# A decoder kernel's first output projection, from one f32 product to three f16 products, with its operands halved during the recurrence solve

## The reference, cut to what matters

```
xn   = rms_norm(x) ; proj = xn @ w_in                      # 1024 -> 3336 columns
y_ssd  = ssd_mixer(proj[:, :1544])                         # 512 columns, a chunked state space mixer
y_rwkv = rwkv7_mixer(proj[:, 1544:])                       # 512 columns, a delta-rule recurrence of 8 heads
mix  = concat(y_ssd, y_rwkv) @ w_out                       # (256 x 1024) @ (1024 x 1024)
h    = x + rms_norm(mix) * post_mix_norm
h    = h + rms_norm(ffn(rms_norm(h)))                      # width 2816, gated, with a short convolution
```

## Time and profile before

| | |
|---|---|
| median of 3 executions | 862.06 us (860.3 to 863.2) |
| the profiled execution | 863.93 us, its span 862.1 us |
| busy, PE / PEld / DVE / ACT / POOL | 815.8 / 688.3 / 565.1 / 391.2 / 71.5 us |
| SP's waits for the first projection's and the second's slots (L438 on L598) | 153.0 us in four waits |
| PE granted clock, stretches of the solve | 0.57 of full in 190 to 194, 1.00 in 174 to 178 |

### The profile page before, as it was taken

One profiled execution on the slowest core, in us unless ns is written; L12 is line 12 of the kernel. 1 busy time (PEld: TensorE's weight loads), 2 busy tenths in 40 slices (PEclk: granted clock), 3 DMA queues, 4 the chain that ended last, 5 costly groups with the idle time before them and its releaser, 6 DMA issues.

```text
span 862.1 us, 17113 instructions
## 1 busy us (share of the span) xinstructions
PE 815.8 (95%) x7466; PEld 688.3 (80%) x7466; DVE 565.1 (66%) x881; ACT 391.2 (45%) x613; POOL 71.5 (8%) x98
## 2 busy tenths in 40 slices
PE   4999978988999999999999999999998999999996
PEld 3798866777767788888886868597886888888885
DVE  2769975645166889999856777567457566674443
ACT  3546351120053376666754764116256356653333
POOL 1123011202000211111000100000200200000000
PEclk9999996998799999999999999979999999999999
DMA  9772230203004745555586256100482516555201
GB/s 329 290 294 98 98 110 2 101 2 102 1 1 156 272 158 196 195 196 197 195 299 240 98 210 227 52 2 0 177 313 99 194 67 227 196 196 209 86 2 49
DMA packets 66491, 127.93 MB, mean 148 GB/s; under 512 B 3696, under 2 KB 27504, under 8 KB 66288
## 3 DMA queue, kind: packets, MB, share of 16 engines
q1 hardware_dynamic: 65104, 122.92, 39.6%
q0 software_dynamic: 592, 2.69, 0.9%
q10 hardware_dynamic: 720, 1.23, 0.4%
HBM read 125.78 MB, written 1.05 MB: 147 GB/s over the span
## 4 chain that ended last, share of the span: by engine, by line
PE 74%; DVE 15%; ACT 6%; issue 2%; DMA 2%; POOL 0%; DVEq 0%; SPq 0%; ACTq 0%
PE bank L493 21%; PE bank L601 18%; DVE arena L481 7%; PE bank L598 6%; PE bank L699 6%; DVE arena L1865 3%; PE bank L1162 3%; PE bank L1953 3%; DMA ring<-in_w_in_dram 2%; ACT arena L472 2%; PE bank L1414 1%; PE bank L1181 1%; PE bank L2335 1%; PE bank L2077 1%; PE bank L2092 1%
## 5 line engine op out<-in xcount | busy, mean ns | idle before, releaser
L481 DVE SCALAR_TENSOR_TENSOR arena<-ring,arena 128x1024 f16<-128x1024 f32 x194 | 229.5, 1230 | 75.7 <-ACT arena L472 75.3
L493 PE MATMUL bank<-hg,arena 128*128 128x256 f16 x2496 | 275.1, 273 | 1.0 <-DVE arena L481 1.0
L493 PEld LDWEIGHTS bank<-hg,arena 128*128 128x128 f16 x2496 | 243.2, 98 | 32.4 <-issue 2.5
L472 ACT ACTIVATE arena<-ring 128x1024 f16<-128x1024 f32 x194 | 191.9, 1045 | 83.5 <-PE bank L601 51.8
L601 PE MATMUL bank<-arena 128*128 128x256 f16 x1296 | 142.2, 273 | 0.2 <-DVE arena L481 0.2
L601 PEld LDWEIGHTS bank<-arena 128*128 128x128 f16 x1296 | 126.6, 98 | 15.5 <-issue 0.9
L598 PE MATMUL bank<-mix,ring 128*128 128x256 f32 x256 | 55.7, 379 | 1.1 <-ACT arena L1797 1.1
L699 PE MATMUL bank<-hg,ring 128*128 128x256 f32 x224 | 51.5, 391 | 4.7 <-DMA ring<-in_w_in_dram 4.7
L598 PEld LDWEIGHTS bank<-mix,ring 128*128 128x128 f32 x256 | 48.5, 190 | 8.4 <-issue 1.9
L699 PEld LDWEIGHTS bank<-hg,ring 128*128 128x128 f32 x224 | 43.7, 197 | 11.4 <-DMA ring<-in_w_in_dram 5.1
L508 ACT ACTIVATE hg<-h,params 128x256 f16<-128x256 f32 (+1 forms) x48 | 23.9, 499 | 56.4 <-DVE h L2281 42.8
(11 more groups left out here) (365 smaller groups left out, 964.7 us busy)
## 6 DMA issues: line engine op xcount, KB each, us to landing
ring<-in_w_in_dram SPq DMA_DIRECT2D x13, 2048.0 KB, 8.7
ring<-in_ffn_w_up_dram SPq DMA_DIRECT2D x22, 1024.0 KB, 7.4
ring<-in_w_ff_dram SPq DMA_DIRECT2D x8, 2048.0 KB, 9.0
ring<-in_w_ff_dram SPq DMA_DIRECT2D x16, 1024.0 KB, 6.0
ring<-in_ffn_w_down_dram SPq DMA_DIRECT2D x11, 1024.0 KB, 6.3
ring<-in_w_out_dram SPq DMA_DIRECT2D x8, 1024.0 KB, 6.3
ring<-in_w_xk_dram SPq DMA_DIRECT2D x2, 2048.0 KB, 12.0
ring<-in_w_xv_dram SPq DMA_DIRECT2D x2, 2048.0 KB, 8.3
```

The costliest lines, as they stand in the source:

```text
L472: nc.scalar.activation(quarter(halves_of(chunk)[0], chunk, q), quarter(slot(*chunk), chunk, q), ACT.Copy, scale=W_SCALE).then_inc(*mark("w ...
L481: nc.vector.scalar_tensor_tensor(quarter(halves_of(chunk)[1], chunk, q), quarter(slot(*chunk), chunk, q), W_SCALE, quarter(halves_of(chunk ...
L493: mm = nc.tensor.matmul(out_, weight[a][:, k, cols], src[:, k, b, :], start=(first and i == 0), stop=(last and i == 2), skip_group_check=True)
```

## The change

The projection `w_out` is now three f16 products per tile, as elsewhere. Its weights are cut in eight row tiles q, each of 128x1024, by `out1_high` (ACT) and `out1_low` (DVE), which stand inside the two chunks of the solve: q = 4c, 4c+1, 4c+2, 4c+3 in chunk c. The halves of q = 0 and 4 go into `hg`, which is free there; those of the others take the place of the f32 words of the tile before, so `out1_high(q)` waits for `out1_low(q - 1)`. ACT's list alternates `mem_high` and `out1_high`. DVE's has `out1_low(4c)` after level 0, `out1_low(4c + 1)` after level 2, `out1_low(4c + 2)` after the 64-wide join, and `out1_low(4c + 3)` after the RK masks. In chunk 1 the mix tiles 0 to 3 are cut as well (`act_mix1_high`, `dve_mix1_low`), into the place of row tile 3. At the end of the recurrence, tiles 4 to 7 are cut from Y: DVE's gate product stays in f32, ACT makes the high half, DVE the low half, the first pair's low half standing inside DVE's work for the second pair. The post norm's root takes the constant that goes with a result 64 times as large.

```diff
--- before.py
+++ after.py
@@ -566,6 +566,45 @@
             mm.then_inc(*mark("column_rstd", n, "column"))
 
 
+        def out1_words(q):
+
+            return ring[:, CHUNK_NO[("w_out", "rows", q // 4)] % RING, 1024 * (q % 4):1024 * (q % 4) + 1024]
+
+        def out1_halves(q):
+
+            kept = hg[:, q:q + 4, :].rearrange("p k t -> p (k t)") if q in (0, 4) else out1_words(q - 1)
+            return kept.bitcast(F16).rearrange("p (w n) -> p w n", w=2)
+
+        def out1_high(act, q):
+            if q % 4 == 0:
+                act.wait_ge(*at("chunk", CHUNK_NO[("w_out", "rows", q // 4)]))
+                act.wait_ge(*at("proj1", PBANKS - 1))
+            else:
+                act.wait_ge(*at("out1 weights low", q - 1))
+            nc.scalar.activation(out1_halves(q)[:, 0, :], out1_words(q), ACT.Copy, scale=W_SCALE).then_inc(
+                *mark("out1_weights_high", "out1 weights high", q))
+
+        def out1_low(dve, q):
+            dve.wait_ge(*at("out1 weights high", q))
+            nc.vector.scalar_tensor_tensor(out1_halves(q)[:, 1, :], out1_words(q), W_SCALE, out1_halves(q)[:, 0, :],
+                                           ALU.mult, ALU.subtract).then_inc(
+                *mark("out1_weights_low", "out1 weights low", q))
+
+        ssd16 = out1_words(3).bitcast(F16).rearrange("p (k w t) -> p k w t", k=4, w=2)
+        mix1_16 = [ssd16[:, k] if k < 4 else mix16[:, k] for k in range(KT)]
+
+        def act_mix1_high(act):
+            act.wait_ge(*at("mix1", 3))
+            act.wait_ge(*at("out1 weights low", 3))
+            nc.scalar.activation(ssd16[:, :, 0, :], mix[:, 0:4, :], ACT.Copy).then_inc(*mark("mix1_high", "mix1 high", 3))
+
+        def dve_mix1_low(dve):
+            dve.wait_ge(*at("mix1 high", 3))
+            nc.vector.tensor_tensor(ssd16[:, :, 1, :], mix[:, 0:4, :], ssd16[:, :, 0, :], ALU.subtract).then_inc(
+                *mark("mix1_low", "mix1 low", 3))
+            for k in range(3):
+                same(("mix1 low", k), ("mix1 low", 3))
+
         def wide(pe, chunk, j, bank, half):
 
             if chunk in SPLIT_NO:
@@ -594,6 +633,11 @@
                 out_, cols = halves(4 + m // 2)[:, m % 2, :], slice(m * P, (m + 1) * P)
                 first = i == order[0] and kk == 0 and m % 2 == 0
                 last = i == order[-1] and kk == min(4, ktiles - 4 * i) - 1
+                if name == "w_out":
+                    for n, (a, b) in enumerate(((0, 0), (1, 0), (0, 1))):
+                        mm = nc.tensor.matmul(out_, out1_halves(k)[:, a, cols], mix1_16[k][:, b, :],
+                                              start=(first and n == 0), stop=(last and n == 2), skip_group_check=True)
+                    return mm
                 if not split:
                     return nc.tensor.matmul(out_, slot(name, "rows", i)[:, kk, cols], src[:, k, :], start=first,
                                             stop=last, skip_group_check=True)
@@ -610,6 +654,8 @@
                 by_rows = n - 2 if tail else n
                 for kk in range(n):
                     pe.wait_ge(*at(*src_ready(4 * i + kk)))
+                    if name == "w_out":
+                        pe.wait_ge(*at("out1 weights low", 4 * i + kk))
                     if split:
                         pe.wait_ge(*at("low", SPLIT_NO[(name, "rows", i)], kk))
                     if kk < by_rows:
@@ -1616,6 +1662,8 @@
                         *mark("solve_vector", "X", c, g, n + 1))
                 if n in (1, 3):
                     mem_low(dve, 4 * c + n // 2 + 2)
+                if n in (0, 2):
+                    out1_low(dve, 4 * c + n // 2)
                 if n == 3:
                     dve_mem_keys(dve, 2 * c)
             for g in range(2):
@@ -1640,6 +1688,7 @@
                                       banks[3 * g][64:128, 0:256].rearrange("p (j m) -> p j m", j=4)).then_inc(
                     *mark("solve_vector", "P64", c, g))
             mem_low(dve, 4 * c + 4)
+            out1_low(dve, 4 * c + 2)
 
             for g in range(2):
                 dve.wait_ge(*at("AK bank", c, g))
@@ -1654,6 +1703,9 @@
                 dve.wait_ge(*at("RK bank", c, g))
                 nc.vector.tensor_tensor(sets[g]["RK"], quarters(3 * g), over(const("incl"), 4), ALU.mult).then_inc(
                     *mark("solve_vector", "RK", c, g))
+            out1_low(dve, 4 * c + 3)
+            if c:
+                dve_mix1_low(dve)
             for g in range(2):
                 dve.wait_ge(*at("RB bank", c, g))
                 nc.vector.tensor_tensor(sets[g]["ARB"], quarters(3 * g + 2), over(const("neg_incl"), 4),
@@ -1670,8 +1722,12 @@
             mem_low(dve, 4 * c + 5)
 
         def act_rwkv_chunk(act, c):
-            for n in range(4 * c + 2, 4 * c + 5):
-                mem_high(act, n)
+            for i in range(3):
+                mem_high(act, 4 * c + 2 + i)
+                out1_high(act, 4 * c + i)
+            out1_high(act, 4 * c + 3)
+            if c:
+                act_mix1_high(act)
             for g in range(2):
                 st = sets[g]
                 act.wait_ge(*at("G bank", c, g))
@@ -1755,6 +1811,13 @@
                     *mark("bonus_vector", *(("bonus products",) if j == 3 else ())))
 
         def dve_rwkv_end(dve):
+            def mix1_low(i):
+                dve.wait_ge(*at("mix1 high", 4 + 2 * i))
+                nc.vector.tensor_tensor(mix16[:, 4 + 2 * i:6 + 2 * i, 1, :], Y[:, 2 * i:2 * i + 2, :],
+                                        mix16[:, 4 + 2 * i:6 + 2 * i, 0, :], ALU.subtract).then_inc(
+                    *mark("rwkv_end_vector", "mix1", 4 + 2 * i))
+                same(("mix1", 5 + 2 * i), ("mix1", 4 + 2 * i))
+
             for i in range(2):
                 dve.wait_ge(*at("mean bank", i))
                 nc.vector.scalar_tensor_tensor(flat(Y)[:, 512 * i:512 * i + 512], banks[4 + i][:, :], -1.0 / RW_HD,
@@ -1772,6 +1835,8 @@
                 dve.wait_ge(*so_far("rwkv_end_vector"))
                 nc.vector.tensor_tensor(flat(Y)[:, s], flat(Y)[:, s], flat(E1)[:, s], ALU.mult).then_inc(
                     *mark("rwkv_end_vector"))
+                if i:
+                    mix1_low(0)
                 dve.wait_ge(*so_far("rwkv_end_vector"))
                 for j in (2 * i, 2 * i + 1):
                     nc.vector.tensor_scalar(Y[:, j, :], Y[:, j, :], par("rwkv_ln_w", j), par("rwkv_ln_b", j),
@@ -1780,10 +1845,9 @@
                 nc.vector.tensor_tensor(flat(Y)[:, s], flat(Y)[:, s], flat(BONUS)[:, s], ALU.add).then_inc(
                     *mark("rwkv_end_vector"))
                 dve.wait_ge(*so_far("rwkv_end_vector"))
-                nc.vector.tensor_tensor(mix[:, 4 + 2 * i:6 + 2 * i, :].rearrange("p a b -> p (a b)"),
-                                        banks[i][:, :], flat(Y)[:, s], ALU.mult).then_inc(
-                    *mark("rwkv_end_vector", "mix1", 4 + 2 * i))
-                same(("mix1", 5 + 2 * i), ("mix1", 4 + 2 * i))
+                nc.vector.tensor_tensor(flat(Y)[:, s], banks[i][:, :], flat(Y)[:, s], ALU.mult).then_inc(
+                    *mark("rwkv_end_vector", "mix1 product", i))
+            mix1_low(1)
 
         def act_rwkv_end(act):
             for i in range(2):
@@ -1796,6 +1860,10 @@
                 act.wait_ge(*at("variance bank", i))
                 nc.scalar.activation(flat(E1)[:, s], banks[6 + i][:, :], ACT.Sqrt, bias=eps[:, 1:2],
                                      scale=1.0 / RW_HD).then_inc(*mark("rwkv_end_act", "variance root", i))
+            for i in range(2):
+                act.wait_ge(*at("mix1 product", i))
+                nc.scalar.activation(mix16[:, 4 + 2 * i:6 + 2 * i, 0, :], Y[:, 2 * i:2 * i + 2, :], ACT.Copy).then_inc(
+                    *mark("mix1_high", "mix1 high", 4 + 2 * i))
 
 
         def hidden16(tiles):
@@ -2528,7 +2596,7 @@
             for c in range(NC_):
                 pe_rwkv_chunk(pe, c)
             pe_rwkv_end(pe)
-            narrow(pe, "w_out", KT, mix, lambda k: ("mix1", k), "out1",
+            narrow(pe, "w_out", KT, None, lambda k: ("mix1 low", k) if k < 4 else ("mix1", k), "out1",
                    lambda b: ("variance root", 1) if b > 1 else ("centred", b))
             pe_mem_values(pe, 0, VALUE_STEPS[:VALUES_AHEAD])
             norm_total(pe, "post_mix", 0, ("mix1", 7))
@@ -2589,7 +2657,7 @@
                 split_high(act, n, range(4))
             post_norm_act(act, "post_mix", "out1")
             split_high(act, SPLIT_1 + 1, (0, 1))
-            norm_root(act, "post_mix", 0)
+            norm_root(act, "post_mix", 0, eps_column=3)
             split_high(act, SPLIT_1 + 1, (2, 3))
             norm_act(act, "pre_ffn", h, "pre_ffn_norm", lambda m: ("post_mix", "added", m), split=True)
             act_mem_values(act, 0)
```

## The result

The changed kernel takes 867.5 us in the median of 13 executions (863.5 to 872.8), the kernel before 860.3 in 13 (853.0 to 863.2); the ratio is 1.0079, with a 95% interval of 1.0053 to 1.0106, so +6.8 us. The change makes the kernel slower by some 0.7%. A ratio here leaves out the slowest executions (over 1.5% above the fastest of their kernel) and is not the quotient of the two medians, which keep them: in the second set the medians, 864.8 and 862.9, are only 2.0 us apart.

What follows compares the result with a forecast made beforehand. PE was taken to bound the projection's end, and a PE, DVE and ACT chain with no full engine the solve. Terms -3.9 + 8.95 - 1.4 + 1.25 = +4.9 on 862.06 gave 867.0 us, range 861.0 to 871.5.

Steps and rivals of the forecast that it cites:

- The projection's own price: First output projection: 192 f16 products in 21.1 us replace 64 f32 products in 27.88, freeing PE of 6.8 us.
- What of it reaches the end: End of the projection: DVE's queue sets the norm's total, so only 3.9 of the 6.8 us are gained.
- The four waits: Solve, after levels 0 and 2 of both chunks: DVE masks queue behind new halves, +2.8, +1.6, +2.65, +1.9, together +8.95 us.
- the prediction's three terms: In the solve: added waits +8.95, stalls giving back -1.4, and the granted clock +1.25 us.
- The late steps: Solve, pieces 2, 3, 6, 7 and the mix: DVE is idle there anyhow, price 0, up to 2.3 + 3.4 us.
- some 9 us later: Sign in the profile after: the projection's first product comes some 9 us later than 247.26.
- What the stalls give back: Solve: PE's unassigned stalls shrink behind the added waits, between 0 and -2.84 us; half taken, -1.4.
- The clock: Solve: the added waits put one more filler on the chain at 1.2 GHz, +1.25 us; bounds -1.26 to +3.8.
- the clock rival: All four fillers behind the waits and the values behind the projection run at low clock: +10.4, 872.5 us; chance 0.11.
- the waits are paid by the stalls: Solve: stalls mostly pay the waits and the clock is kind, +0.95, 863.0 us, no measurable change; 0.21 with half-way cases.
- The faster rival: Solve: new halves are ready when DVE comes, so only the projection counts, -3.9, 858.2 us; chance 0.05.

Runs made afterwards that it cites:

- second set: The changed kernel run again without edit (again_after), twelve executions, against the kernel before: ratio 1.0058.
- e5_end_only: Changed kernel with only the end reordered: ACT makes seven of eight splits before the last mix products, DVE sums after six splits; ratio 1.0042 to the kernel before.
- e2_halves_only: Kernel before plus only the eight pairs of weight-half steps, results unused, projection still f32; ratio 1.0112 to the kernel before.
- e1_order: Changed kernel with ACT's list in the solve turned round, each new high half ahead of the mem half; 858.7 us, ratio 0.9962 to the kernel before.
- e6_values_ahead: e1_order with six instead of two steps of memory values ahead of the norm's total; 854.4 us, ratio 0.9923 to the kernel before.
- e7_idle_filled: e1_order plus twelve useless f16 products on PE ahead of the norm's total; 858.7 us, ratio 0.9982 to the kernel before.
- e8_end_and_values: Changed kernel with e1_order's exchange, e5_end_only's end and four steps of values ahead of the total; 853.7 us, ratio 0.9927 to the kernel before.
- e3_lows_later: Changed kernel with DVE's four early low halves one level later, behind the mem low halves; 860.4 us, ratio 0.9982 to the kernel before.
- again_before: The kernel before run again without edit, for a second profile; 862.1 us, ratio 0.9994.
- again_after: The changed kernel run again without edit, for a second profile; 864.8 us, ratio 1.0058 to the kernel before.
- e9: Changed kernel with ACT's order turned round only for the first piece of each chunk (q = 0 and 4); 860.5 us, ratio 1.0005 to the kernel before.
- e10: Changed kernel with ACT's order turned round only for the second piece of each chunk (q = 1 and 5); 858.9 us, ratio 0.999 to the kernel before.

## Why the forecast came out

The forecast was +4.9 us, from 867.0 against 862.06; measured were +6.8 (4.6 to 9.1 by the interval), and in the second set +5.0. Step by step:

**The projection's own price, -6.8.** 21.0 us in place of 27.88, 6.9: as worked out.

**What of it reaches the end, -3.9.** Measured -3.7 (25.66 against 29.37) in every profile with this end. The mechanism was the one named: DVE's eight splits behind the mix's last low half, sums right behind, PE idle. e5_end_only moved the total 2.6 us by DVE's and ACT's order alone.

**The four waits, +8.95.** They stand where the prediction put them. Idle times of 2.67, 2.75 and 2.76 were given as 2.7, that of 4.07 as "some 4". The first can be priced by itself: from the solve's first product to the mask it takes 9.22 us in both profiles of the kernel before, 11.98 and 11.99 in those of the changed kernel, +2.8 as worked out. From there on waits, stalls and clock mix. e2_halves_only has the waits, with what stalls and clock add to them, and nothing of the new end: it costs 9.7 us, beside the 8.8 of the prediction's three terms. The profiles without any wait have a solve of 94.5 to 98.6 us (both of the kernel before, e1_order, e6_values_ahead, e7_idle_filled, e8_end_and_values) or 100.4 (e3_lows_later), the four with all waits 103.8 to 108.3.

The late steps (pieces 2, 3, 6, 7 and the mix) were priced at 0, and in chunk 0 that held: from the filler of level 3 to the first product of chunk 1 it is 23.7 us before and 23.6 after, with that filler at the low clock in both; and e1_order, which has all of these steps, has a solve of 98.3. The sign "some 9 us later" for the projection's first product came out as 4.9 in the first profile and 8.6 in the second.

**What the stalls give back, -1.4.** Mis-sized. All three stalls (0.56, 0.78, 1.50) are gone in the changed kernel's two traces, and at the same three places e1_order has 0.66, 0.50 and 1.50 again. The second profile of the kernel before has 0.15, 1.05 and 0.66 there, so the term was -1.9 to -2.8, not one fixed number. That a wait ahead of a stall swallows it is what the traces show; what ends such a stall no row shows. But the places are fixed: from one stall of chunk 0 to the next it is 128 products (43 + 12 + 64 + 9, then 55 + 12 + 61), each with its own weight load, in every trace that has them. The Trainium skill ("Runtime: NRT & Kernel Launch", The launch sequence) has instructions fetched ahead autonomously. By that rule, which gave the whole -2.84, the first pair of traces agrees; the second profile of the kernel before had only 1.86 to give.

**The clock, +1.25.** Mis-sized, and its second part is the reason that the sum came out low. Two parts. In the solve, the mean of the four profiles with all waits is 106.3, that of the two of the kernel before 97.6: +8.7, where the terms for the solve (8.95 - 1.4 + 1.25) gave 8.8. That it was met so closely is luck: the stalls gave back more than forecast and the clock took more. With the stalls at -1.9 to -2.8 the clock's part is then about +1.6 to +2.6 instead of 1.25. The traces also show it by itself, in the filler (12 products, 1.48 us at 2.4 GHz, 2.74 at 1.2) that stands right behind each of the four places:

| us of the filler | chunk 0, level 1 | chunk 0, level 3 | chunk 1, level 1 | chunk 1, level 3 | sum |
|---|---|---|---|---|---|
| before | 1.48 | 2.61 | 1.48 | 2.17 | 7.7 |
| again_before | 1.48 | 1.48 | 2.74 | 1.65 | 7.4 |
| changed kernel | 2.74 | 2.55 | 2.74 | 2.53 | 10.6 |
| again_after | 2.74 | 2.51 | 2.60 | 2.30 | 10.2 |
| e2_halves_only | 2.74 | 2.74 | 2.74 | 2.74 | 11.0 |
| e5_end_only | 2.74 | 2.74 | 2.73 | 2.74 | 11.0 |

Behind a wait the filler ran at a granted clock of 0.50 to 0.61, 16 times of 16 (of the four in e9 and e10 three took 2.57 or 2.74 us, one 1.77), which costs 3.1 us more than in the two profiles of the kernel before. With that the terms of the solve come to 9.2 to 10.2 where 8.7 were measured, so some 0.5 to 1.5 us stay unassigned. In chunk 0, level 1, the eight profiles without a wait there all have 1.48 or 1.49. Behind the projection, the idle PE lets the clock fall in some executions: total to total took 20.48 in one profile of the changed kernel and 23.33 in the other, and in the six profiles with the 3.25 us gap (both of these, e1_order, e3_lows_later, e9, e10) 20.48, 20.48, 22.04, 23.26, 23.33 and 23.48, a mean of 22.2, +1.7. In the four where the gap was filled or short (e5, e6, e7, e8) the products of the total took 1.03 to 1.10 us, the price at 2.4 GHz. I had this effect only in the clock rival, with the right place, at 1.7 where a whole fall costs 3.0. The Trainium skill ("TensorE: Matmul & The Clock Gate", HAM oscillation) says that an idle gap between matmul groups throttles the clock and the next group starts cold; by that rule the trace agrees where the gap was 3.25 us, in four profiles of six.

With the terms as measured, 8.7 in the solve, -3.7 at the end and +1.7 behind it, the sum is +6.7, beside the 6.8 of the ratio. That these means over a few profiles come so near is luck in good part: single solves differ by 4.6 us, and the sum leaves out all behind the next norm's total, where no edit reaches. That stretch took 565.0 and 564.9 us in the kernel before, 563.4 and 563.3 in the changed one, and 560.0 to 565.5 over all runs. The profiles' own spans, 860.9 and 865.0 in the mean, are 4.1 apart.

**The rivals.** That the waits are paid by the stalls was half right: the stalls were paid in full, and it wasn't enough. The clock rival had the mechanism right in the solve: all four fillers behind the waits ran at the low clock. It had the price wrong, 5.0 us for them where 3.1 came of it, since some of these fillers were at the low clock before as well (2.61, 2.17 and 2.74 in the table). Its +10.4 was not reached, though the slowest execution (872.75) is at its 872.5. The faster rival, halves that are ready when DVE comes, is no property of the changed kernel, but it is exactly what e1_order makes of it: the prediction gave it 858.2, and it took 858.7.

The mean granted clock of the whole solve would not have shown what the waits do to it: 0.81 to 0.86 with all waits, 0.84 to 0.88 without, ranges that overlap; the fillers right behind the waits do. What stays open is why the clock is low at some other places in one execution and not in the next, and, after e7_idle_filled, what the clock behind the projection is worth over many executions.

## What to carry to other kernels

When work is slipped into another engine's idle time, look at what stands in front of it in both queues: here the new DVE step waited for an ACT step that stood behind one that waited for PE, and an exchange of two lines was worth more (1.0 to 1.2%) than the faster product itself (6.8 us, 0.8%). A product made cheaper gives only what the next engine in line lets through, so the order of the next engine's list (and what PE can do meanwhile) belongs to the same change. And one profile of each kernel may be a pair from opposite ends of their spreads: compare structure in them, and sums in many executions.

## What the runs showed that was not expected

The stalls of PE in runs of tiny products (0.15 to 1.5 us with no releaser, 128 products apart) go when waits of 2 to 4 us come between them: of the four or five in a solve of the kernel before at most one was left (0.68 and 0.94 in two profiles, none in two), and without the waits three to five are back. And the filler behind each such wait ran at 1.2 GHz, 16 times of 16. And the same idle 3.25 us of PE let the clock fall in four profiles and not in two; when it fell, four f32 products took 2.05 instead of 1.10 us, and the stretch behind was up to 3.0 us longer.
